# RWKV state products alternate between two banks, and the output projection's half rows move between them

## The reference

```python
def _rwkv7_step(state, inp):
    r, w, k, v, kk, kka = inp
    sa = jnp.einsum('dbhvk,dbhk->dbhv', state, kk)
    state = state * w[..., None, :] - sa[..., :, None] * kka[..., None, :] + v[..., :, None] * k[..., None, :]
    y = jnp.einsum('dbhvk,dbhk->dbhv', state, r)
    return state, y
...
    mix = jnp.concatenate([y_att, y_rwkv], axis=-1) @ w_out[l]
    h = h + _rmsnorm(mix, mix_post_g[l])
```

## Time and profile before

| | |
|---|---|
| median of 3 runs | 1148.49 us (1148.44 to 1150.95) |
| the profiled execution: its span | 1147.7 us |
| median less span (what lies around it) | 0.8 us |
| PE busy (matmul) | 1140.1 us, 99% |
| PE weight loads busy | 1066.7 us, 93% |
| GpSimd, ScalarE, VectorE busy | 907.8, 630.0, 551.1 us |
| granted clock | 1.00 in every stretch of the stage |
| first and last product of L1310 | 879.5 and 934.4 us |

### The profile page before, as it was taken

One profiled execution on the slowest core, in us unless ns is written; L12 is line 12 of the kernel. 1 busy time (PEld: TensorE's weight loads), 2 busy tenths in 40 slices (PEclk: granted clock), 3 DMA queues, 4 the chain that ended last, 5 costly groups with the idle time before them and its releaser, 6 DMA issues.

```text
span 1147.7 us, 24129 instructions
## 1 busy us (share of the span) xinstructions
PE 1140.1 (99%) x10058; PEld 1066.7 (93%) x10058; DVE 551.1 (48%) x982; ACT 630.0 (55%) x1003; POOL 907.8 (79%) x700
## 2 busy tenths in 40 slices
PE   9999999999999999999999999999999999999998
PEld 9998999999998999998999999999889989999997
DVE  5543575642652223223644233568966766333333
ACT  6666676447644554454744444689653337444443
POOL 6987667875986999988799999698562036999994
PEclk9999999999999999999999999999999999999999
DMA  7655445654665656656466656664700035655662
GB/s 284 193 168 180 129 130 164 205 163 151 188 222 195 202 188 189 188 186 184 166 186 188 188 191 185 202 193 148 213 3 3 14 103 182 185 184 184 187 190 101
DMA packets 53660, 192.43 MB, mean 168 GB/s; under 512 B 6320, under 2 KB 7216, under 8 KB 53168
## 3 DMA queue, kind: packets, MB, share of 16 engines
q1 hardware_dynamic: 51824, 184.36, 51.7%
q10 hardware_dynamic: 1728, 6.53, 1.6%
HBM read 188.77 MB, written 1.05 MB: 165 GB/s over the span
## 4 chain that ended last, share of the span: by engine, by line
PE 96%; DVE 1%; POOL 1%; ACT 1%; DMA 0%; issue 0%; DVEq 0%; POOLq 0%; ACTq 0%
PE product L591 19%; PE product L593 18%; PE product L592 18%; PE bank L721 7%; PE bank L723 7%; PE bank L722 7%; PE bank L1236 3%; PE product L1310 2%; PE product L1236 1%; PE product L820 1%; PE product L749 1%; PE product L822 1%; PE product L821 1%; PE bank L778 1%; POOL weight_lo L551 1%; PE bank L1071 0%
## 5 line engine op out<-in xcount | busy, mean ns | idle before, releaser
L551 POOL TENSOR_TENSOR weight_lo<-raw_ring,weight_hi 128x512 fp32r<-128x512 f32 x684 | 892.3, 1336 | 191.0 <-ACT weight_hi L2619 177.3
L2619 ACT ACTIVATE weight_hi<-raw_ring 128x1024 fp32r<-128x1024 f32 x338 | 356.7, 1059 | 358.0 <-DMA raw_ring<-in_ffn_gu 109.8
L591 PE MATMUL product<-operand_B_hi,weight_hi 128*128 128x256 f32 x1104 | 312.0, 283 | 0.2 <-POOL weight_lo L551 0.2
L593 PE MATMUL product<-operand_B_hi,weight_lo 128*128 128x256 f32 x1104 | 310.8, 282 | 0.0
L592 PE MATMUL product<-operand_B_lo,weight_hi 128*128 128x256 f32 x1104 | 310.5, 281 | 0.0
L591 PEld LDWEIGHTS product<-operand_B_hi,weight_hi 128*128 128x128 f32 x1104 | 207.8, 188 | 3.3 <-POOL weight_lo L551 0.4
L592 PEld LDWEIGHTS product<-operand_B_lo,weight_hi 128*128 128x128 f32 x1104 | 207.9, 188 | 3.1
L593 PEld LDWEIGHTS product<-operand_B_hi,weight_lo 128*128 128x128 f32 x1104 | 207.8, 188 | 0.0
L591 PE MATMUL product<-operand_A_hi,weight_hi 128*128 128x256 f32 x712 | 203.8, 286 | 0.1
L592 PE MATMUL product<-operand_A_lo,weight_hi 128*128 128x256 f32 x712 | 200.4, 281 | 0.0
L593 PE MATMUL product<-operand_A_hi,weight_lo 128*128 128x256 f32 x712 | 200.4, 281 | 0.0
(11 more groups left out here) (428 smaller groups left out, 1517.0 us busy)
## 6 DMA issues: line engine op xcount, KB each, us to landing
raw_ring<-in_w_in SPq DMA_DIRECT2D x95, 512.0 KB, 3.6
raw_ring<-in_ffn_gu SPq DMA_DIRECT2D x88, 512.0 KB, 3.5
raw_ring<-in_ffn_down SPq DMA_DIRECT2D x44, 512.0 KB, 3.5
raw_ring<-in_w_mlp_up SPq DMA_DIRECT2D x32, 512.0 KB, 3.6
raw_ring<-in_w_mlp_down SPq DMA_DIRECT2D x32, 512.0 KB, 3.5
raw_ring<-in_w_out SPq DMA_DIRECT2D x14, 512.0 KB, 3.6
raw_ring<-in_w_gmlp_v SPq DMA_DIRECT2D x8, 512.0 KB, 3.5
raw_ring<-in_w_branch_c SPq DMA_DIRECT2D x8, 512.0 KB, 3.6
```

Source lines behind the costliest of these rows:

```text
L551: last = k.nc.gpsimd.tensor_tensor(k.wlo[:, slot, part], k.raw[:, slot, part], k.whi[:, slot, part].bitcast(F32), ALU.subtract)
L591: mm(ps, w_hi, op.hi[:, b, :], start=b == 0, stop=False)
L593: return mm(ps, w_lo, op.hi[:, b, :], start=False, stop=b == blocks - 1)
L2619: k.nc.scalar.activation(k.whi[:, slot, 0:w], k.raw[:, slot, 0:w], ACT.Copy).then_inc(k.s["hi_ready"], 1)
```

## The change

Only the TensorE program changes; the number of products and matmuls stays. Inside `from_state` and `to_state` products into `chain_bank` and into `y_bank` now take turns in pairs, an opposite pair of one bank beside a same pair of the other. Each piece has one wait on `half_mm` in its middle, for the last product of its first part. `from_state` waits for `y_taken` at its start now. `x_mm` and `ss_mm`, which release ScalarE and VectorE, come with the last product into `chain_bank`, which is now at or next to the end of the piece. Around chunks 2 and 3 the half rows are dealt out anew. The diff:

```diff
@@ -1315,50 +1315,58 @@
 
         if j:
             pe.wait_ge(s["ss_ev"], j)
+            pe.wait_ge(s["y_taken"], j)
         else:
             pe.wait_ge(s["s_red"], ATT_HEADS)
+            pe.wait_ge(s["o_ev"], ATT_HEADS)
         x, y, z, aq, st = k.chain_bank, k.y_bank, k.z4[j], k.aq, k.st
-        for h in range(2):
+
+        def right_of_values(h, b, d):
+            r = half(1 - d)
+            return product(x, d, 4 * h + b, z[r, d, h, b, 0, :], r, values_of(j, d)[r, b, h, :],
+                           start=h + b == 0, stop=j == 0 and h == 1 and b == AB - 1)
+
+        def right_of_state(h, b, d, stop=False):
+            r = half(h)
+            return product(x, d, 4 * h + b, aq[r, d, chunk(d, j), b, 0, :], r, st[r, 4 * d + b, :], stop=stop)
+
+        def outputs_of_values(h, b, d, start=False):
+            r = half(1 - d)
+            return product(y, h, 4 * d + b, z[r, d, h, b, 1, :], r, values_of(j, d)[r, b, h, :], start=start)
+
+        def outputs_of_state(h, b, d):
+            r = half(h)
+            return product(y, h, 4 * d + b, aq[r, d, chunk(d, j), b, 1, :], r, st[r, 4 * d + b, :])
+
+        for b in range(AB):
+            for d in range(2):
+                right_of_values(0, b, d)
+            for d in range(2):
+                last = outputs_of_values(1 - d, b, d, start=b == 0)
+        for b in range(AB):
+            for d in range(2):
+                last_x = right_of_values(1, b, d)
+            if j:
+                for h in range(2):
+                    last = outputs_of_state(h, b, 0)
+        if j:
             for b in range(AB):
                 for d in range(2):
-                    r = half(1 - d)
-                    last = product(x, d, 4 * h + b, z[r, d, h, b, 0, :], r, values_of(j, d)[r, b, h, :],
-                                   start=h + b == 0, stop=j == 0 and h == 1 and b == AB - 1)
-        if j == 0:
-            last.then_inc(s["x_mm"], 1)
+                    last_x = right_of_state(1 - d, b, d)
+                for h in range(2):
+                    last = outputs_of_state(h, b, 1)
+            block_end(last_x)
         else:
-            for b in range(AB):
+            last_x.then_inc(s["x_mm"], 1)
+        pe.wait_ge(s["half_mm"], block_end(last))
+        for b in range(AB):
+            if j:
                 for d in range(2):
-                    h, r = 1 - d, half(1 - d)
-                    last = product(x, d, 4 * h + b, aq[r, d, chunk(d, j), b, 0, :], r, st[r, 4 * d + b, :])
-            x_block = block_end(last)
+                    last_x = right_of_state(d, b, d, stop=b == AB - 1)
+            for d in range(2):
+                last = outputs_of_values(d, b, d)
         if j:
-            pe.wait_ge(s["y_taken"], j)
-        else:
-            pe.wait_ge(s["o_ev"], ATT_HEADS)
-        for b in range(AB):
-            for d in range(2):
-                r = half(1 - d)
-                last = product(y, d, 4 * d + b, z[r, d, d, b, 1, :], r, values_of(j, d)[r, b, d, :], start=b == 0)
-        y_block[0] = block_end(last)
-        if j:
-            pe.wait_ge(s["half_mm"], x_block)
-            for b in range(AB):
-                for d in range(2):
-                    r = half(d)
-                    last = product(x, d, 4 * d + b, aq[r, d, chunk(d, j), b, 0, :], r, st[r, 4 * d + b, :], stop=b == AB - 1)
-            last.then_inc(s["x_mm"], 1)
-        pe.wait_ge(s["half_mm"], y_block[0])
-        for b in range(AB):
-            for d in range(2):
-                r = half(1 - d)
-                last = product(y, 1 - d, 4 * d + b, z[r, d, 1 - d, b, 1, :], r, values_of(j, d)[r, b, 1 - d, :])
-        if j:
-            for d in range(2):
-                for b in range(AB):
-                    for h in range(2):
-                        r = half(h)
-                        last = product(y, h, 4 * d + b, aq[r, d, chunk(d, j), b, 1, :], r, st[r, 4 * d + b, :])
+            last_x.then_inc(s["x_mm"], 1)
         y_block[0] = block_end(last)
 
     def solve(j):
@@ -1370,40 +1378,44 @@
     def to_state(j):
 
         pe.wait_ge(s["sa_ev"], j + 1)
-        state, y, z, sa = k.chain_bank, k.y_bank, k.z4[j], k.sa
-        if j + 1 < NRC:
-            tok = k.tok[j]
+        state, y, z, sa, onward = k.chain_bank, k.y_bank, k.z4[j], k.sa, j + 1 < NRC
+        tok = k.tok[j] if onward else None
+
+        def state_of_values(h, b, d, start=False):
+            r = half(1 - d)
+            return product(state, h, 4 * d + b, tok[r, d, b, h, :], r, values_of(j, d)[r, b, h, :], start=start)
+
+        def state_of_solution(h, b, d, stop=False):
+            r = half(d)
+            return product(state, h, 4 * d + b, tok[r, d, b, h, :], r, sa[r, 4 * h + b, :], stop=stop)
+
+        def outputs_of_solution(h, b, d, stop=False):
+            r = half(d)
+            return product(y, h, 4 * d + b, z[r, d, h, b, 1, :], r, sa[r, 4 * h + b, :], stop=stop)
+
+        pe.wait_ge(s["half_mm"], y_block[0])
+        for b in range(AB):
+            if onward:
+                for d in range(2):
+                    state_of_values(d, b, d, start=b == 0)
+            for d in range(2):
+                last = outputs_of_solution(d, b, d)
+        if onward:
             for b in range(AB):
                 for d in range(2):
-                    r = half(1 - d)
-                    product(state, d, 4 * d + b, tok[r, d, b, d, :], r, values_of(j, d)[r, b, d, :], start=b == 0)
+                    last = state_of_solution(1 - d, b, d)
+        pe.wait_ge(s["half_mm"], block_end(last))
+        for b in range(AB):
+            if onward:
+                for d in range(2):
+                    state_of_values(1 - d, b, d)
+            for d in range(2):
+                last = outputs_of_solution(1 - d, b, d, stop=b == AB - 1)
+        if onward:
             for b in range(AB):
                 for d in range(2):
-                    r = half(d)
-                    last = product(state, 1 - d, 4 * d + b, tok[r, d, b, 1 - d, :], r, sa[r, 4 * (1 - d) + b, :])
-            s_block = block_end(last)
-        pe.wait_ge(s["half_mm"], y_block[0])
-        for b in range(AB):
-            for d in range(2):
-                r = half(d)
-                last = product(y, 1 - d, 4 * d + b, z[r, d, 1 - d, b, 1, :], r, sa[r, 4 * (1 - d) + b, :])
-        y_block[0] = block_end(last)
-        if j + 1 < NRC:
-            pe.wait_ge(s["half_mm"], s_block)
-            for b in range(AB):
-                for d in range(2):
-                    r = half(1 - d)
-                    product(state, 1 - d, 4 * d + b, tok[r, d, b, 1 - d, :], r, values_of(j, d)[r, b, 1 - d, :])
-            for b in range(AB):
-                for d in range(2):
-                    r = half(d)
-                    last = product(state, d, 4 * d + b, tok[r, d, b, d, :], r, sa[r, 4 * d + b, :], stop=b == AB - 1)
-            last.then_inc(s["ss_mm"], 1)
-        pe.wait_ge(s["half_mm"], y_block[0])
-        for b in range(AB):
-            for d in range(2):
-                r = half(d)
-                last = product(y, d, 4 * d + b, z[r, d, d, b, 1, :], r, sa[r, 4 * d + b, :], stop=b == AB - 1)
+                    last_state = state_of_solution(d, b, d, stop=b == AB - 1)
+            last_state.then_inc(s["ss_mm"], 1)
         last.then_inc(s["yy_mm"], 1)
 
     pe.wait_ge(s["evacuated"], k.segs["qk"].slot + 8)
@@ -1505,19 +1517,20 @@
         level_both(2, level)
         level_both(3, level)
     half_row(0)
+    from_state(2)
     half_row(1)
-    from_state(2)
     solve(2)
     half_row(2)
     to_state(2)
     half_row(3)
-    half_row(4, slice(0, 1))
     from_state(3)
+    half_row(4)
     solve(3)
-    half_row(4, slice(1, 2))
+    half_row(5, slice(0, 1))
     feature_major(0)
     to_state(3)
-    for n in range(5, 2 * AB):
+    half_row(5, slice(1, 2))
+    for n in range(6, 2 * AB):
         half_row(n)
 
 
```

## The result

The changed kernel takes 1151.39 us in the median of 20 runs (1149.55 to 1153.13), the kernel before 1149.77 in 20 runs beside it. The ratio is 1.0017, 95% interval 1.0011 to 1.0023: 1.6 us slower, inside the 0.3% that I had called no change, and outside the range that I gave. All medians here are of fast runs: one slow run of after_shifted (4608.94 us) is left out, and repeated was run once.

A forecast was written before the change was run, and what follows sets the result against it. The prediction took TensorE, busy for 99% of the span, as the bound. 3.75 us gained up to the last start of `solve(2)`, less 0.3 lost behind it, gave 3.5 off 1148.5: 1145.0 us, range 1143.6 to 1150.6.

The forecast's parts named there:

- the pace and the drain: In `from_state` and `to_state`: 14.5 ns a matmul on four quarters of the array, and about 0.3 us for each drain.
- The first rival: `from_state`/`to_state`: pace over four quarters not kept; 18 to 24 ns, chance 0.20 (shared); 25 ns, 2.1 us slower, 0.10.
- `from_state(1)` gives its 1.4 us: Chunk 1: the piece takes 2.15 us against 3.56, and the gain counts since DVE has been waiting for PE there.
- `from_state(0)` gains 0.35: Level 1: of 0.45 us saved only 0.35 are left, since `level_left(3, 1)` needs a transpose that ends at 883.32.
- the 0.5 us of `to_state(1)`: Chunk 1: the piece takes 2.15 us against 2.63, and its gain of 0.5 us reaches the end.
- Level 2: `to_state(0)` saves 0.5 us, but `ss_mm` comes later and PE needs DVE's transpose, so 0.1 us is kept.
- T: The last start of `solve(2)`, at 920.12 before; forecast 3.75 us of gain up to there, with DVE late from there on.
- Behind T: `from_state(3)` at T + 7.35, last start of `to_state(3)` at T + 15.3, `feature_major(1)` at T + 21.9; 0.3 us lost.
- the case that the prediction had set aside with a gain of 4.5 us: If DVE gets in before GpSimd (margin 0.2 us), L2449 takes 0.69 us and the gain is 4.5 us.
- 7.4 us: Stated total of the savings in the `from_state` and `to_state` pieces, of which part does not reach the end.

The follow-up runs named there:

- after_shifted: The changed kernel with 128 do-nothing instructions (256 satisfied waits) added in `branch_b`, far ahead of the levels; -1.5 us against the kernel before, ratio 0.9978 to 0.9996.
- repeated: after_shifted with the first 64 matmuls of `from_state(2)` issued 8 times in place of once; +14.6 us against the kernel before, one run.
- all_row_shifted: after_shifted with quarter rows of out_2 ahead of `from_state(3)`, between its parts and ahead of `solve(3)`; -3.0 us against the kernel before, ratio 0.9961 to 0.9983.
- products_shifted: The changed kernel's alternating products with the half rows of before, plus 128 do-nothing instructions in `branch_b`; -0.4 us against the kernel before, ratio 0.9986 to 1.0004.
- before_shifted: The kernel before with 128 do-nothing instructions (256 satisfied waits) added in `branch_b`; -0.3 us against the kernel before, ratio 0.9990 to 1.0008.
- before_waits: The kernel before with 128 satisfied waits (64 instructions) added in levels 2 to 5; +4.5 us against the kernel before, ratio 1.0026 to 1.0052.
- after_block: The changed kernel with 512 satisfied waits (256 instructions, one whole block) added in `branch_b`; +14.3 us against the kernel before, ratio 1.0110 to 1.0137.

## Why the prediction was wrong

**Right: the pace and the drain.** The 128 matmuls of `from_state(2)` "in one block of about 2.4 us (2.15 and the last one's 0.22) with 15 or 16 in flight": it is 2.44 us, and a window of 20 ns at 914.90 has 16. The first 96 take 1.41 us, forecast 1.39. Drains are 0.29 to 0.33 us. `from_state(2)` gave 1.34 us from first to last start (forecast 1.4), `to_state(2)` 0.47 (0.5). The first rival is refuted as a slower pace. The Trainium skill ("TensorE: Matmul & The Clock Gate", section "Wait — 56ns, not 53.3ns?") has no start-to-start under some 25 ns; the 14.8 ns over 96 matmuls on four quarters of the array disagree.

**Wrong: "`from_state(1)` gives its 1.4 us".** It ended at 898.37 against 898.35 before; the hole took all of it. This is the step that failed. The prediction put the supply of instructions at nothing: it took 14.5 ns a matmul for as long as products last, while blocks of 256 instructions in a row come every 3.75 us, 29.3 ns a matmul. I had read 28 ns in the earlier trace rows as the pace of two quarters alone, and it also stands next to that limit. The rival's words, that "the sequencer may not deliver", named the place, but I gave it the form of an even 20 or 25 ns. It comes as full pace and then a hole, whose place hangs on the count of instructions since the program's start. The Trainium skill ("Runtime: NRT & Kernel Launch", section "Instruction fetch mechanics") says that blocks are 16 KiB of 256 instructions, fetched while the one before runs, and that this is mostly hidden. Size and count agree with the trace. Hidden it is only while blocks last some 3.7 us, taken over a few of them.

**Wrong: `from_state(0)` gains 0.35.** It waits for attention's last output at its front now ("L2381" above, 0.58 us). `to_state(0)` began 0.22 us later, at 888.59. I had moved the wait for `o_ev` with the rest and not asked when its release comes. Of the 0.5 us of `to_state(1)` the third hole, in level 4, took 0.3. Level 2 went about as forecast (0.3 us where 0.1 was kept): `level_left(2, 2)` waits for L2453 and begins at 892.98.

**T** came 1.19 us sooner (918.94 for 920.12), not 3.75: `half_row(0)` 0.2 sooner, `from_state(2)` 1.34, less 0.35 for one more switch to rows, which the sum did not have.

**Behind T.** `from_state(3)` began at T + 6.59, not at 7.35. VectorE was on time to 0.05 us and was not held up:

```profile
923.17 0.69 DVE L2460 TENSOR_TENSOR arena<-product,arena 128x512 f32<-128x512 f32 x1 [5.61 <-PE product L1310]
923.90 0.69 DVE L2462 TENSOR_TENSOR arena<-arena,small 128x512 f32<-128x512 f32 x1
...
926.24 1.72 DVE L2492 TENSOR_TENSOR pre<-pre,small 128x512 f32<-128x512 f32 x1
```

This is the case that the prediction had set aside with a gain of 4.5 us. GpSimd's subtraction began at 924.91, T + 5.98 and not T + 4.78, and L2492 took 1.72 us beside it. It did not stay tied to T. `half_row(1)`, moved behind `from_state(2)`, also frees the ring's place for the first half of that weight tile: SyncE asked for it at 918.11 in place of 915.73, and for the second half at 919.20, T + 0.26 as before. ScalarE could begin on the tile at 923.78, where before had 923.76. No run tested that the late first half is the reason. Then the hole of 1.69 us took that and more: `to_state(3)`'s last start is at T + 16.2 (forecast 15.3), `feature_major(1)` at T + 22.8 (21.9).

**The sum.** With the holes nearly gone, after_shifted has 3.06 us less in L + R than before, where I forecast 3.5. The holes are what the prediction lacked: after has 3.34 us of them and after_shifted 0.36, and L + R differs by 3.1. In the profiled executions they cancel the gain. That the rest comes so near is in part luck. Up to `half_row(0)` the forecast was 2.35 us and after_shifted has 1.5, the best of its four like executions; behind it the forecast was 1.1 and it has 1.5, since VectorE was not held up. (The "7.4 us" that the prediction starts from is a slip: its pieces add up to 6.0. Nothing else was worked out from it.) Why the median of after lies 1.8 us above its profiled run is not shown; that holes of the same code vary (0.36 to 1.9 us in the levels of after_shifted, repeated, all_row_shifted and products_shifted) is the nearest to a cause that the runs have.

## What to carry to other kernels

Short matmuls have a second pace, that of their instructions: 14.6 ns each here over blocks in a row, whatever the array could do. Before packing them closer, count the instructions from the ends of the blocks of 256, with the slow work among them, and ask how long each block lasts. Here one of 3.0 us behind one of 4.0 passed, one of 2.5 behind one of 4.0 did not, and near a weight tile a block took up to 5 us to come. If a hole "issue" appears that no semaphore explains, move it with instructions that do nothing in a stretch of long matmuls before redesigning anything: the same change was 1.6 us slower or 1.5 us faster than before by the phase alone. What it is worth at one phase says little about another, and any edit ahead of it moves the phase.

## What the runs showed of the hardware that I had not expected

- An instruction of two satisfied waits on TensorE costs nothing that can be measured behind long matmuls, up to 16 of them for a tile (before_shifted), and 68 ns among 64x64 ones (before_waits, 4.35 us for 64).
- Behind the bursts of repeated the granted clock fell. By stretch, three holes and the rows behind them:

```profile
918.25:921.98 3.73, 2.12 (x128) 1.99 (x128) 0.00 (x0) 0.00 (x0) 0.00 (x0) 1.00 0.02 4
921.99:925.73 3.74, 2.13 (x128) 1.99 (x128) 0.00 (x0) 0.00 (x0) 0.00 (x0) 1.00 0.02 4
927.00:931.00 4.00, 3.92 (x45) 2.71 (x42) 0.00 (x0) 0.60 (x1) 0.00 (x0) 0.57 0.01 4
```

From 927 to 931 it is 0.57, mostly the 1.2 GHz level, and the rows of `half_row(1)` start 0.43 us apart in place of 0.23. No hole of the other kernels in this stage did that (the longest is 2.73 us, in after_block), nor did the one of 2.40 us later in repeated.
